# A decoder step with product-key experts: the boundaries between the stages of the expert part are rearranged

## The reference

```python
def chunk_fn(xc):                      # peer(), 8 heads, top 16 of 128 x 128 product keys
    q = (xc @ w_query).reshape(PEER_CHUNK, PEER_HEADS, D_QUERY)
    s1 = einsum('chk,nk->chn', q[..., :HALF_Q], k1)
    s2 = einsum('chk,nk->chn', q[..., HALF_Q:], k2)
    v1, i1 = top_k(s1, 16); v2, i2 = top_k(s2, 16)
    sc, ci = top_k(v1[..., :, None] + v2[..., None, :], 16)      # over 256 sums
    eid = e1 * N_KEYS + e2                                        # the chosen experts
    gate = softmax(sc)
    act = gelu(einsum('chkd,cd->chk', exp_u[eid], xc))
    return einsum('chk,chkd->cd', gate * act, exp_v[eid])
...
x = x + peer(rms_norm(x));  y = rms_norm(x, final_g)
```

## Time and profile before

| | |
|---|---|
| median of 3 runs | 1872.55 us (1871.93 to 1876.08) |
| the profiled execution | 1874.36 us, of which span 1872.4 us |
| mean granted clock of PE | 0.984 |
| PE busy | 1776.9 us, 95% of the span |
| DVE busy | 1405.0 us, 75% |
| ACT busy | 627.9 us, 34% |
| POOL busy | 401.1 us, 21% |
| read from HBM, written to it | 343.75 MB, 35.34 MB |

### The profile page before, as it was taken

One profiled execution on the slowest core, in us unless ns is written; L12 is line 12 of the kernel. 1 busy time (PEld: TensorE's weight loads), 2 busy tenths in 40 slices (PEclk: granted clock), 3 DMA queues, 4 the chain that ended last, 5 costly groups with the idle time before them and its releaser, 6 DMA issues. The chain is left out here.

```text
span 1872.4 us, 27294 instructions
## 1 busy us (share of the span) xinstructions
PE 1776.9 (95%) x9385; PEld 1552.0 (83%) x9385; DVE 1405.0 (75%) x2984; ACT 627.9 (34%) x1030; POOL 401.1 (21%) x478
## 2 busy tenths in 40 slices
PE   7998989899999899889999999999999999998997
PEld 6776654576766587779989989999999999998997
DVE  5887551299999677857878878778878887875766
ACT  5223451211111466633323323333333333322332
POOL 1000000022323100024434434333323323320000
PEclk9999999999999899989999999999999999999999
DMA  7315502322211256478989879988889889874544
GB/s 258 113 60 207 201 1 107 116 69 68 70 56 57 71 211 232 168 276 281 306 271 318 286 260 301 314 263 300 302 273 318 299 282 310 286 250 151 158 144 150
DMA packets 203178, 382.11 MB, mean 204 GB/s; under 512 B 14447, under 2 KB 141965, under 8 KB 199981
## 3 DMA queue, kind: packets, MB, share of 16 engines
q1 hardware_dynamic: 166197, 246.39, 39.5%
q0 software_dynamic: 36864, 134.23, 20.5%
HBM read 343.75 MB, written 35.34 MB: 202 GB/s over the span
## 5 line engine op out<-in xcount | busy, mean ns | idle before, releaser
L1477 PE MATMUL bank<-p_high,v_high 128*128 128x416 f32 x896 | 316.6, 353 | 11.7 <-DVE v_low L1944 9.5
L1477 PE MATMUL bank<-p_high,v_low 128*128 128x416 f32 x896 | 317.8, 355 | 0.0
L1477 PE MATMUL bank<-p_low,v_high 128*128 128x416 f32 x896 | 314.4, 351 | 0.0
L1425 PE MATMUL bank<-h_high,u_high 128*128 128x416 f32 x768 | 272.4, 355 | 15.6 <-DVE u_low L1944 14.9
L1425 PE MATMUL bank<-h_high,u_low 128*128 128x416 f32 x768 | 272.6, 355 | 0.0
L1425 PE MATMUL bank<-h_low,u_high 128*128 128x416 f32 x768 | 270.0, 352 | 0.0
L1710 POOL DMA_INDIRECT rows<-in_u_rows,row_u x128 | 170.1, 1329 | 263.4 <-DVE dots L2032 194.9
L1615 ACT CAST p_high<-gel 128x416 fp32r<-128x416 f32 x128 | 69.1, 540 | 414.9 <-DVE gel L1989 404.0
L1710 POOL DMA_INDIRECT rows<-in_v,row_u x128 | 145.7, 1139 | 290.9 <-DVE y L2027 225.1
L1944 DVE TENSOR_TENSOR v_low<-vv,v_high 128x1024 fp32r<-128x1024 f32 x112 | 137.2, 1225 | 75.4 <-ACT v_high L1609 75.0
L1412 PE MATMUL bank<-h2T,early 128*128 128x416 f32 x512 | 184.5, 515 | 1.4 <-ACT gel L1556 1.4
(11 more groups left out here) (235 smaller groups left out, 2868.2 us busy)
## 6 DMA issues: line engine op xcount, KB each, us to landing
vv<-in_v SPq DMA_DIRECT2D x112, 512.0 KB, 6.9
u<-in_uT SPq DMA_DIRECT2D x96, 512.0 KB, 5.0
gates_kept<-staged SPq DMA_DIRECT2D x13, 2048.0 KB, 7.5
gate<-gates_kept SPq DMA_DIRECT2D x30, 832.0 KB, 9.2
early<-in_uT SPq DMA_DIRECT2D x32, 512.0 KB, 3.6
w_in_sb<-in_w_in SPq DMA_DIRECT2D x9, 1024.0 KB, 8.2
wq<-in_w_q SPq DMA_DIRECT2D x16, 512.0 KB, 3.6
u<-in_v SPq DMA_DIRECT2D x16, 512.0 KB, 4.1
```

The source lines that it names most:

```text
L1425: ins = pe.matmul(a_ps[par][:, 0:DT], x[:, par, k], y, start=(k == 0 and n == 0), stop=(k == KT - 1 and n == 2))
L1477: ins = pe.matmul(out, x[:, c, at:at + P], y, start=(opens and c == 0 and n == 0), stop=(closes and c == CG - 1 and n == 2))
```

## The change

Five things are rearranged; the arithmetic stays the same.

1. PE turns the slots (`turn_slots`) ahead of the last early chunk behind the heads (chunk 21) instead of behind it. DVE does the sum, reciprocal and product of the gates before it takes the keys, not after.
2. DVE splits h behind the last batch of gates instead of before batch 47; u's first split stays. The first split chunk does the products without h_low first and waits for the parts of h_low one by one.
3. SP waits for the stored gates ahead of the first load of v, no longer ahead of the loads of u.
4. Pieces 2 and 3 of v of group 23 go to u's places too (WIDE = 23), one group sooner.
5. `gates_kept` is ordered by group: a store writes, for each partition, 32 runs of 512 B, and a load of one group reads one run of 6656 B from each of 128 partitions. Before, a store wrote one run of 16 KB per partition and a load read 13 x 128 runs of 512 B.

```diff
-        gates_kept = nc.dram_tensor("gates_kept", (NB, P, NK, GB), F32, kind="Internal").ap()
+        gates_kept = nc.dram_tensor("gates_kept", (NG, P, NB, CG * GB), F32, kind="Internal").ap()
...
-                               not fetch, not fetch and GROUPS * part + gg > WIDE)
+                               not fetch, not fetch and GROUPS * part + gg > WIDE + 1)
...
-        WIDE = GROUPS * (PARTS - LEAD)
-        def wide(part):
-            return isinstance(part, int) and part >= PARTS - LEAD
+        WIDE = GROUPS * (PARTS - LEAD) - 1
+        def wide(part, gg):
+            return isinstance(part, int) and GROUPS * part + gg >= WIDE
...
-                sp.dma_start(gates_kept[b], staged[:, b % 2]).then_inc(gates_stored[b % 2], 16)
+                sp.dma_start(gates_kept[:, :, b].rearrange("g p n -> p g n"),
+                             staged[:, b % 2].rearrange("p (g c) t -> p g (c t)", c=CG)).then_inc(gates_stored[b % 2], 16)
...
-            for b in range(2):
-                sp.wait_ge(gates_stored[b], 16 * ((NB + 1 - b) // 2))
-
             def load_v(part, gg, m):
                 g = GROUPS * part + gg
-                if wide(part) and m >= 2:
+                if isinstance(part, int) and g == m == 0:
+                    for b in range(2):
+                        sp.wait_ge(gates_stored[b], 16 * ((NB + 1 - b) // 2))
+                if wide(part, gg) and m >= 2:
                     sp.wait_ge(a_done, NK)
                     if g > WIDE:
                         sp.wait_ge(v_done, KT // VS * (VS * (g - 1) + m + 1))
...
-                src = gates_kept[:, :, bass.ds(CG * g, CG), :].rearrange("b k c t -> k b (c t)")
-                sp.dma_start(gate[:, gg % 2].rearrange("k b c t -> k b (c t)"), src).then_inc(gate_in[gg % 2], 16)
+                src = gates_kept[bass.ds(g, 1)].rearrange("o k b n -> (o k) (b n)")
+                sp.dma_start(gate[:, gg % 2].rearrange("k b c t -> k (b c t)"), src).then_inc(gate_in[gg % 2], 16)
...
             def activate(q, par):
                 pe.wait_ge(u_split, q - EARLY + 1)
                 wait(pe, acted, q - 1)
-                if isinstance(q, int) and q == EARLY:
-                    pe.wait_ge(h_split, KT)
-                for k in range(KT):
+                first = isinstance(q, int) and q == EARLY
+                order = [(k, n) for k in range(KT) for n in (0, 1, 2)]
+                if first:
+                    order = [x for x in order if x[1] != 1] + [x for x in order if x[1] == 1]
+                for z, (k, n) in enumerate(order):
                     high, low = h_high[:, k], h_low[:, k, P:T]
-                    for n, (x, y) in enumerate(((u_high, high), (u_high, low), (u_low, high))):
-                        ins = pe.matmul(a_ps[par][:, 0:DT], x[:, par, k], y,
-                                        start=(k == 0 and n == 0), stop=(k == KT - 1 and n == 2))
+                    if first and n == 1:
+                        pe.wait_ge(h_split, k + 1)
+                    x, y = ((u_high, high), (u_high, low), (u_low, high))[n]
+                    ins = pe.matmul(a_ps[par][:, 0:DT], x[:, par, k], y, start=(z == 0), stop=(z == len(order) - 1))
                 ins.then_inc(a_done, 1)
...
+            def turn_slots():
+                pe.wait_ge(decoded, 4 * PH)
+                pe.wait_ge(s_taken, TILES * PH)
+                for n in range(3):
+                    if n == 2:
+                        pe.wait_ge(gates, 2)
...
             for n in range(PH):
                 head(n)
                 for q in early_after(n):
+                    if q == EARLY - IN_GATES - 1:
+                        turn_slots()
                     activate_early(q)
...
             for n in range(BATCHES):
                 if n == SPLIT_AT:
-                    dve.wait_ge(a_done, EARLY)
-                    split_h()
                     split_u(EARLY, 0)
...
+            dve.wait_ge(a_done, EARLY)
+            split_h()
```

More of the change, by code:

```diff
@@ L1214, in piece_in @@
             g = GROUPS * part + gg
-            if not wide(part):
+            if not wide(part, gg):
                 return v_in[m % 2], 16 * (VS // 2 * g + m // 2 + 1)
@@ L1301, in load_v @@
                         sp.wait_ge(v_done, KT // VS * (VS * (g - 1) + m + 1))
-                elif wide(part) and g > WIDE:
+                elif wide(part, gg) and g > WIDE:
                     sp.wait_ge(v_done, KT // VS * (VS * (g - 1) + m + 1))
@@ L1419, in activate @@
                 wait(pe, acted, q - 1)
-                if isinstance(q, int) and q == EARLY:
-                    pe.wait_ge(h_split, KT)
-                for k in range(KT):
+                first = isinstance(q, int) and q == EARLY
[3 more added lines that the diff above has]
+                for z, (k, n) in enumerate(order):
                     high, low = h_high[:, k], h_low[:, k, P:T]
-                    for n, (x, y) in enumerate(((u_high, high), (u_high, low), (u_low, high))):
-                        ins = pe.matmul(a_ps[par][:, 0:DT], x[:, par, k], y,
-                                        start=(k == 0 and n == 0), stop=(k == KT - 1 and n == 2))
+                    if first and n == 1:
+                        pe.wait_ge(h_split, k + 1)
+                    x, y = ((u_high, high), (u_high, low), (u_low, high))[n]
+                    ins = pe.matmul(a_ps[par][:, 0:DT], x[:, par, k], y, start=(z == 0), stop=(z == len(order) - 1))
                 ins.then_inc(a_done, 1)
+            def turn_slots():
[4 more added lines that the diff above has]
+                        pe.wait_ge(gates, 2)
+                    for i in range(TILES):
+                        r = ROWS[i]
+                        src = ef[0:r, n, i] if n < 2 else tops[0:r, i]
+                        dst = banks[n][:, i * P:(i + 1) * P] if i < 4 else banks[3 + n // 2][:, n * NS:(n + 1) * NS]
+                        ins = pe.transpose(dst, src.rearrange("p h k -> p (h k)"), ident[0:r, 0:r])
+                    ins.then_inc(slot_turned, 1)
             for n in range(PH):
@@ L1907, in take_slots @@
                 nc.vector.tensor_copy(dst[:, SEQ:T], banks[3 + n // 2][:, n * NS:(n + 1) * NS]).then_inc(slot_taken, 1)
[L1909 to L1914, removed]
             dve.wait_ge(gate_exp, 1)
@@ L1929, in _ @@
             nc.vector.tensor_copy(w0[:], flat(tops[:, 0]))
+            dve.wait_ge(slot_turned, 2)
+            take_slots(0, e1T)
+            take_slots(1, e2T)
+            dve.wait_ge(slot_taken, 2)
+            nc.vector.tensor_copy(e1b[:], e1T[:, P:T]).then_inc(keys_made, 1)
+            nc.vector.tensor_copy(e2b[:], e2T[:, P:T]).then_inc(keys_made, 1)
             dve.wait_ge(slot_turned, 3)
```

## The result

The changed kernel takes 1851.72 us (median; 1848.75 to 1853.27) against 1872.24 us for the kernel before: ratio 0.9888, 95% interval 0.9863 to 0.9913. It is 20.5 us faster, where I had forecast 14.8. The profiled execution took 1853.27 us, its span 1851.3 us.

A forecast was written before the change was run, and what follows sets the result against it. PE was taken to bound the long stage, with gains where stages meet: 3.9 + 4.0 + 1.6 + 1.0 + 4.3 = 14.8 us, giving 1857.8 us against a median of 1872.55; range 1849 to 1867.

The forecast's parts named there:

- rival (b): No clock fall at first and third boundary, stores cost nothing, 3 us of mid-stage idle go: 1849 us; chance 0.13.
- First boundary: Start of the gates stage: slots turned before chunk 21 and gates before keys on DVE gain 3.9 us.
- h split last: End of the gates stage: taking eight splits out of DVE's chain to the last placed batch gains 4.0 us.
- u not behind the stores: Start of the next stage: the third chunk's u, issued without waiting for the last store, gains 1.6 us.
- Rival (c): Row chain, started by the last store, gives u's gain back at the first part's end: 1860.4 us; chance 0.08.
- Stores, S = 9.5 us: Stores of gates in 512 B runs: S, the time one store takes, is 9.5 us, bounds 7.5 and 12.8.
- (a): Stores of gates near the upper bound, u later than now and last blocks wait: 1864.7 us; chance 0.15.
- (d): Slower: a store of 512 B runs takes longer than a block; 1895 us at S = 16; chance 0.05.
- 11.1 - S: Gain in us at the third chunk's start, where S is the time a store of gates takes.
- Shorter loads in the long stage: Loads of gates relieve the DMA engines where PE idles 12.5 us: 1 us gained, bounds 1 lost and 5 gained.
- Third boundary: Five pieces of v, two in u's places, take 26.7 us in place of 31.01: 4.3 us gained.

The follow-up runs named there:

- e9: Changed kernel with DVE's eight splits of h before batch 47 again: 1853.2 us, ratio 0.9898.
- e3: Changed kernel with SP's wait for the stores ahead of the loads of u again: 1850.4 us, ratio 0.9890.
- e1: The changed kernel again with no edit: 1851.35 us, ratio 0.9884.
- e11: e8 with SP's wait for the stores ahead of the loads of u again: 1843.5 us, ratio 0.9860.
- e8: Changed kernel with ACT's copies of h and first hot batch ahead of the gelu of chunk 21: 1842.9 us, ratio 0.9847.
- e2: Changed kernel with gates_kept ordered by block as before: 1857.65 us, ratio 0.9923.
- e5: Kernel before with only gates_kept ordered by group: 1866.15 us, ratio 0.9971.
- e6: Changed kernel with the old gates_kept layout, loading only the first of 13 blocks of each group's gates (others stale): 1845.4 us, ratio 0.9869.
- e4: Changed kernel with two pieces of v in u's places only from group 24 on, as before: 1858.4 us, ratio 0.9923.

## Why the prediction was right, and where its sum was not

The direction and the range held (1849 to 1867). That 1851.7 lies within it is partly luck. The low end was rival (b), and two of (b)'s three conditions were not met as stated: the clock did fall at the first boundary, and the long stage gave 9.2 us in place of 3. (Its sum also counts those 3 us on top of the forecast's 1.0; in place of it they give 1850.) By the prediction's own steps:

- **First boundary, 3.9 us:** right, with the reason. The gates came early, ACT's queue became the last wait (the hot batch is ready 14.0 us after the exponentials), the clock fell. Measured 4.3 us at the first product and 3.7 at the half chunk, since the clock was 0.58 there in place of 0.64.
- **h split last, 4.0 us:** right; e9 takes it away alone and the stage starts 3.9 us later.
- **u not behind the stores, 1.6 us:** right at the third chunk (1.7), with no gain for the kernel that could be measured (e3 is 0.9 us faster than e1, e11 0.6 us slower than e8). I had followed the gain no further than the third chunk. In e3 none of it is left at the fifth, in e11 against e8 all of it and more. Rival (c) named such a loss, though by the row chain at the end of the part; in e3 it occurs within the first group.
- **Stores, S = 9.5 us:** 7.9 in the median, against 7.5 before. Runs of 512 B cost a typical 2 MB store 0.4 us, not 2. Only the last store took 9.4 us, and in the kernel before the last took 8.5, as the earlier trace rows showed, where I put in 7.5 for the old form. The u of the third chunk hangs on just this last store, so the term hit (1.7 for 1.6) although the price per run was wrong: that is luck. In e2 the last store takes 8.5, and the same formula, 11.1 - S, gives 2.6 where 2.7 was measured. Why the last store takes longer in both forms is not shown. Rivals (a) and (d) needed stores of over 12 us; none came. The Trainium skill's three cycles of overhead per packet ("DMA: Bandwidth & Descriptors", "Why small descriptors are slow (HBM only)") had led to 8.9 as an estimate; the measured 7.9 is below it too.
- **Shorter loads in the long stage, 1.0 us (bounds 1 lost and 5 gained):** this is the term that was mis-sized. It gave 9.2 us in the profiles, in medians 6.3 net of the later fifth chunk (e2) and 5.6 (e5). The mechanism was named rightly, and e6 shows it. The row that I had gave the ceiling, 12.5 us of idle time, and I took 1 us of it without tying each of the waits to a transfer. The loads of 9.2 us in the earlier trace rows were a sign, with the DMA engines 0.87 busy: the same 832 KB landed after 7.0 us once the runs were long. The upper bound should have been the whole idle time and the clock behind it (e6 has 2.7 us idle and 836.6 busy, for 12.5 and 840.7 before).
- **Third boundary, 4.3 us:** it gave 7.0 in the first profile and 8.6 in e1 (the rest takes 183.1 and 181.6 us there, 190.2 before and 191.6 in e4; 180.5 to 184.1 in all others where WIDE is 23). The waits were right (4.2 for 4.2), and so nearly were the five pieces, 26.3 us for 26.7. The step that fell short is the clock: I counted one fall and kept it in both kernels, and stopped at the fifth piece. In the kernel before a second fall followed the third wait, mean clock 0.74 from 1713.44 to 1720.00, about 1.7 us, and it is gone. The fall that I kept does not always come either: without it, as in e1, the five pieces take 24.7 us, which is what rival (b) had said of this boundary.

Taken away one at a time, the parts come to 6.3 (layout) + 7.1 (wide) + 1.8 (h) + 1.7 (slots) - 0.9 (u) = 16 us, and all together to 20.4. The difference is within what medians with intervals of 2.5 to 5 us to either side can say; that the parts help each other is not shown.

## What to carry to other kernels

When a stage is bound by one engine but the DMA engines are 0.87 busy, its few short waits can have one cause: count the runs of each transfer, not only its bytes. Here it paid to put the long runs on the side that is read during the busy stage. Follow a gain past the point where it appears, to the next wait behind it, two chunks on in this case, and read that wait from more than one execution. A fall of the clock behind a short wait came in some executions and not in others: price it with and without. After a reorder ask which queue the next wait hangs on: ACT's was idle for 6.75 us ahead of work that needed nothing of what it waited for, and filling that gave 8.5 us more.

## What the runs showed of the hardware

- A 2 MB store to HBM in 4096 runs of 512 B landed after a median of 7.9 us (7.8 to 9.4), one in 128 runs of 16 KB after 7.5 (6.6 to 8.5, e2). A load of 832 KB, among other traffic, took a median of 9.4 us in 1664 runs of 512 B (e2) and 7.0 us in 128 runs of 6656 B. Short runs cost the store little and the load much; whether that is the direction or the traffic beside it was not tried.
- A wait of PE can cost more than its own length. After the 5.14 us wait at the first boundary the next 32 matmuls took 6.29 us at a granted clock of 0.58, between the levels of 1.2 and 2.4 GHz; in e8, with no wait ahead, they took 3.82. Short waits can do it too: behind a wait of 1.91 us at the third boundary of the kernel before, 26 matmuls took 6.56 us at 0.74, where 4.9 us is usual (24 take 4.53).
- The length of a short wait does not tell whether the clock falls. Behind waits of 1.82 us (changed kernel) and 2.20 us (before, at 829.26) it was 0.73 over the next 6.3 us; behind 1.79 us (e1, the same kernel and place) and 2.42 us (e5) it stayed at 1.00. Where it fell, the piece of 24 matmuls behind it took 6.2 us, where it did not, 4.6.
